# Second norm of an encoder layer: g applied to the gathered rows instead of before the split, half of the split on VectorE, the last residual ahead of it

## The reference

```
h = rmsnorm(x, norm_ffn_g)          # x * rsqrt(mean(x^2) + eps) * g
grp_logits = h @ w_grp + b_grp      # 4 groups, top 1
exp_logits = h @ w_exp + b_exp      # 8 experts in the group, top 2
y = sum over the chosen experts e of weight * ((silu(h @ w_gate[e]) * (h @ w_up[e])) @ w_down[e])
x = x + y;  out = rmsnorm(x, final_norm_g)
```

## Time and profile before

| | before |
|---|---|
| runs (us) | 861.05, 861.25, 862.1; median 861.25 |
| profiled execution, span from first to last instruction (us) | 857.0 |
| busy: TensorE, VectorE, ScalarE, GpSimd (us) | 763.1, 224.5, 163.3, 63.6 |
| mean granted TensorE clock (share of full) | 0.972 |
| moved by DMA | 238.90 MB |

### The profile page before, as it was taken

How to read it: one execution, slowest core, us unless ns; L and a number is a source line. 1 busy time by engine, 2 the same in 40 slices (tenths; PEclk the granted TensorE clock), 3 DMA queues, 4 the chain that set the end, 5 groups by cost and what they waited for, 6 DMA issues and landing times.

```text
span 857.0 us, 14144 instructions
## 1 busy us (share of the span) xinstructions
PE 763.1 (89%) x6112; PEld 378.4 (44%) x6112; DVE 224.5 (26%) x429; ACT 163.3 (19%) x315; POOL 63.6 (7%) x49
## 2 busy tenths in 40 slices
PE   6997999999999997799999999999999988988830
PEld 3443444464566555444444444444444334334310
DVE  3037544003355257411111111111111101111116
ACT  5244120014344254201010101010101000000004
POOL 0714000000000034100000000000000000000023
PEclk9999999999999998899999999999999999999975
DMA  9322020402450362499999999999999999999945
GB/s 330 77 98 98 1 99 1 148 1 81 177 216 2 117 275 99 169 395 417 420 420 416 420 419 418 420 418 418 419 417 420 419 417 421 418 418 420 416 169 227
DMA packets 54011, 238.90 MB, mean 279 GB/s; under 512 B 5856, under 2 KB 7264, under 8 KB 37600
## 3 DMA queue, kind: packets, MB, share of 16 engines
q1 hardware_dynamic: 47712, 225.93, 65.5%
q10 hardware_dynamic: 5120, 8.39, 2.6%
q0 software_dynamic: 1152, 4.19, 1.4%
HBM read 228.02 MB, written 10.49 MB: 278 GB/s over the span
## 4 chain that ended last, share of the span: by engine, by line
PE 58%; SPq 16%; DMA 14%; DVE 6%; ACT 3%; issue 2%; POOL 1%; POOLq 0%; ACTq 0%; DVEq 0%
PE bank L408 17%; SPq L321 13%; PE bank L700 13%; DMA arena<-in_w_up 9%; PE bank L719 7%; PE bank L690 6%; PE bank L569 4%; DMA arena<-in_w_down 3%; PE bank L620 3%; DVE arena L998 2%; SPq L332 2%; PE bank L603 2%; PE bank L511 1%; DMA arena<-rows_out,arena 1%; PE bank L587 1%
## 5 line engine op out<-in xcount | busy, mean ns | idle before, releaser
L700 PE MATMUL bank<-arena 128*64 128x512 f32 x1024 | 227.9, 594 | 14.0 <-DMA arena<-in_w_up 13.2
L408 PE MATMUL bank<-arena 128*128 128x512 f32 x384 | 171.0, 601 | 5.9 <-ACT arena L799 5.9
L700 PEld LDWEIGHTS bank<-arena 128*64 128x64 f32 x1024 | 73.5, 137 | 162.4 <-issue 137.7
L719 PE MATMUL bank<-arena 128*64 128x512 f32 x512 | 116.9, 598 | 15.7 <-ACT arena L952 15.1
L408 PEld LDWEIGHTS bank<-arena 128*128 128x128 f32 x384 | 72.2, 191 | 94.5 <-issue 90.5
L690 PEld LDWEIGHTS bank<-arena 128*128 128x128 bf16 x3072 | 92.3, 98 | 25.2 <-issue 25.2
L690 PE MATMUL bank<-arena 128*128 128x64 bf16 x3072 | 96.0, 194 | 0.0
L998 DVE TENSOR_TENSOR arena<-bank,arena 128x256 f32<-128x256 f32 (+1 forms) x80 | 30.3, 395 | 249.3 <-ACT arena L948 214.1
L719 PEld LDWEIGHTS bank<-arena 128*64 128x64 f32 x512 | 34.5, 136 | 77.6 <-issue 62.1
L948 ACT ACTIVATE arena<-bank 128x256 f32<-128x256 f32 x32 | 12.3, 384 | 284.8 <-PE bank L700 284.8
L1273 DVE COPY arena<-bank 128x512 f32<-128x512 f32 x32 | 22.1, 692 | 120.7 <-PE bank L719 120.7
(11 more groups left out here) (157 smaller groups left out, 506.0 us busy)
## 6 DMA issues: line engine op xcount, KB each, us to landing
arena<-in_w_gate SPq DMA_DIRECT2D x64, 1024.0 KB, 23.3
arena<-in_w_up SPq DMA_DIRECT2D x64, 1024.0 KB, 23.1
arena<-in_w_down SPq DMA_DIRECT2D x32, 2048.0 KB, 26.1
arena<-in_w_in SPq DMA_DIRECT2D x6, 2048.0 KB, 8.1
rows_out<-arena ACTq DMA_DIRECT2D x64, 128.0 KB, 6.1
arena<-in_x SPq DMA_DIRECT2D x4, 512.0 KB, 5.9
arena<-in_w_out SPq DMA_DIRECT2D x2, 1024.0 KB, 8.0
arena<-in_w_out SPq DMA_DIRECT2D x1, 2048.0 KB, 18.3
```

The costliest lines, as they stand in the source:

```text
L408: m = pe.matmul(pbank[n % UNIT_BANKS][:], lhs(k), rhs(k), start=(k == 0), stop=(k == KC - 1))
L700: mm = pe.matmul(pbank[s][64 * half:64 * half + 64, :].rearrange("p (g f) -> p g f", g=2), xT[:, k], wg_sb[s][:, :, k, half * 256:(half + ...
L719: mm = pe.matmul(pbank[5 + s][64 * half:64 * half + 64, :], hidT[:, kc % 2, kc // 2], wd_sb[s][:, kc, half * 512:(half + 1) * 512], start= ...
```

## The change

g is no longer multiplied into the rows before the split. The split works on x1 * rstd2 alone, and g, now laid out by chunk as gffn_pk (128 x 8, loaded in place of g2b), is multiplied in when the gathered rows leave PSUM (`rows_T_evict`; ScalarE does the same in the general path). hi is an Identity activation of x1 with scale rstd2; h2 as a tile is gone. The rest, x1 * rstd2 - hi, is made on VectorE by scalar_tensor_tensor, into rest2, which lies by chunk; mid and the last part read it in unit step. GpSimd keeps the last part alone. Tile 3 is split in two halves. On VectorE the order is new: rest(0), rest(1) between the first tiles' steps, route(0, 2) ahead of x1_T_evict(2), residual(3) and norm2(3) behind it, then rest(2). On TensorE router(1) stands ahead of out_proj(3, 0) and the numbers of keep_clock differ. The gather goes tile by tile, with one start flag for the bank. SP waits for the same number of parts as before.

```diff
-        h2 = [at(128 + 4 * i, D) for i in range(2)]
+        rest2 = [at(128 + 4 * i, KC, P) for i in range(2)]
...
-            sp.dma_start(g2b, g_ffn.broadcast_to((P, D))).then_inc(g2_in, 16)
+            sp.dma_start(gffn_pk, g_ffn.rearrange("l (p k) -> (l p) k", k=KC)).then_inc(g2_in, 16)
...
             router(0)
             x1_T(1)
             out_proj(2, 1)
+            router(1)
             out_proj(3, 0)
-            router(1)
             x1_T(2)
             out_proj(3, 1)
             router(2)
-            keep_clock(4)
             x1_T(3)
-            keep_clock(4)
+            keep_clock(3)
             router(3)
-            keep_clock(10)
+            keep_clock(12)
...
-                for k in range(KC):
-                    for t in range(TT):
+                for t in range(TT):
+                    for k in range(KC):
                         for i in range(3):
                             mm = pe.matmul(pbank[3][:, k * SLOTS:(k + 1) * SLOTS], h2_part[t][i][:, k], pick[s][:, t],
-                                           start=(t == 0 and i == 0), stop=(t == TT - 1 and i == 2))
+                                           start=(t == 0 and k == 0 and i == 0), stop=(t == TT - 1 and k == KC - 1 and i == 2))
...
-            def hi(t):
+            def hi(t, ks):
                 act.wait_ge(sumsq2_done, t + 1)
-                act.wait_ge(h2_done, t + 1)
-                nc.scalar.copy(h2_part[t][0], h2_by_chunk(t)).then_inc(hi_done, 1)
-
-            def mid(t):
-                act.wait_ge(rest_done, t + 1)
-                nc.scalar.copy(h2_part[t][1], h2_by_chunk(t)).then_inc(mid_done, 1)
-
-            for stage, t in ((square, 0), (square_root, 0), (square, 1), (x1_T_evict, 0), (hi, 0), (square_root, 1),
-                             (x1_T_evict, 1), (mid, 0), (hi, 1), (square, 2), (square_root, 2), (mid, 1), (x1_T_evict, 2),
-                             (hi, 2), (mid, 2), (square, 3), (x1_T_evict, 3), (square_root, 3), (hi, 3), (mid, 3)):
-                stage(t)
+                act.wait_ge(rstd2_done, t + 1)
+                nc.scalar.activation(h2_part[t][0][:, ks], x1_by_chunk(t)[:, ks], ACT.Identity,
+                                     scale=rstd2[:, t:t + 1]).then_inc(hi_done, 1)
+
+            def mid(t, ks, rests):
+                act.wait_ge(rest_done, rests)
+                nc.scalar.copy(h2_part[t][1][:, ks], rest2[t % 2][:, ks]).then_inc(mid_done, 1)
+
+            square(0)
+            square_root(0)
+            square(1)
+            x1_T_evict(0)
+            hi(0, all_k)
+            square_root(1)
+            x1_T_evict(1)
+            hi(1, all_k)
+            mid(0, all_k, 1)
+            mid(1, all_k, 2)
+            square(2)
+            square_root(2)
+            hi(2, all_k)
+            x1_T_evict(2)
+            square(3)
+            x1_T_evict(3)
+            square_root(3)
+            hi(3, halves[0])
+            mid(2, all_k, 3)
+            hi(3, halves[1])
+            mid(3, halves[0], 4)
+            mid(3, halves[1], 5)
...
-                dve.wait_ge(rstd2_done, t + 1)
-                if t >= 2:
-                    dve.wait_ge(parts_done, t - 1)
-                nc.vector.scalar_tensor_tensor(h2[t % 2], x1[:, t], rstd2[:, t:t + 1], g2b, ALU.mult, ALU.mult).then_inc(h2_done, 1)
...
+            def rest(t, ks, his):
+                dve.wait_ge(rstd2_done, t + 1)
+                dve.wait_ge(hi_done, his)
+                if t >= 2:
+                    dve.wait_ge(parts_done, t - 1)
+                nc.vector.scalar_tensor_tensor(rest2[t % 2][:, ks], x1_by_chunk(t)[:, ks], rstd2[:, t:t + 1],
+                                               h2_part[t][0][:, ks], ALU.mult, ALU.subtract).then_inc(rest_done, 1)
+
             residual(0)
             norm2(0)
             residual(1)
             x1_T_evict(0)
             norm2(1)
+            rest(0, all_k, 1)
             x1_T_evict(1)
+            rest(1, all_k, 2)
             residual(2)
             norm2(2)
+            route(0, 2)
             x1_T_evict(2)
-            route(0, 2)
             residual(3)
+            norm2(3)
+            rest(2, all_k, 3)
             x1_T_evict(3)
-            norm2(3)
+            rest(3, halves[0], 4)
+            rest(3, halves[1], 5)
             route(2, 4)
-            dve.wait_ge(mid_done, TT)
-            ks = slice(KC // 2, KC)
-            tt(h2_part[TT - 1][2][:, ks], h2_by_chunk(TT - 1)[:, ks], h2_part[TT - 1][1][:, ks],
-               ALU.subtract).then_inc(parts_done, 1)
...
-                nc.vector.tensor_copy(xT.rearrange("p k t -> p (k t)"), pbank[3][:]).then_inc(xt_evicted, 1)
+                tt(xT, pbank[3][:].rearrange("p (k t) -> p k t", k=KC), gffn_pk.unsqueeze(2).broadcast_to((P, KC, SLOTS)),
+                   ALU.mult).then_inc(xt_evicted, 1)
...
-            for t in range(TT):
-                pool.wait_ge(hi_done, t + 1)
-                nc.gpsimd.tensor_tensor(h2_by_chunk(t), h2_by_chunk(t), h2_part[t][0], ALU.subtract).then_inc(rest_done, 1)
+            for t in range(TT - 1):
                 pool.wait_ge(mid_done, t + 1)
-                ks = slice(0, KC if t < TT - 1 else KC // 2)
-                nc.gpsimd.tensor_tensor(h2_part[t][2][:, ks], h2_by_chunk(t)[:, ks], h2_part[t][1][:, ks],
-                                        ALU.subtract).then_inc(parts_done, 1)
+                nc.gpsimd.tensor_tensor(h2_part[t][2], rest2[t % 2], h2_part[t][1], ALU.subtract).then_inc(parts_done, 1)
+            for h in range(2):
+                pool.wait_ge(mid_done, TT + h)
+                nc.gpsimd.tensor_tensor(h2_part[TT - 1][2][:, halves[h]], rest2[(TT - 1) % 2][:, halves[h]],
+                                        h2_part[TT - 1][1][:, halves[h]], ALU.subtract).then_inc(parts_done, 1)
```

More of the change, by code:

```diff
@@ L138, in mixer_and_moe @@
         w_lr = at(206, KC, 2 * RANK)
-        g2b = at(199, D)
         gfb = at(128, D)
@@ L154, in mixer_and_moe @@
         b_r_sb = take(GROUPS + EXPERTS)
-        gffn = take(KC)
+        gffn, gffn_pk = take(KC), take(KC)
         ssq, root, rstd = take(TT), take(TT), take(TT)
@@ L242, in mixer_and_moe @@
         wo_done, x1_done, sumsq2_done, ms2_done = sem("wo_done"), sem("x1_done"), sem("sumsq2_done"), sem("ms2_done")
-        root2_done, rstd2_done, h2_done = sem("root2_done"), sem("rstd2_done"), sem("h2_done")
+        root2_done, rstd2_done = sem("root2_done"), sem("rstd2_done")
         xr_done, res_pool = sem("xr_done"), sem("res_pool")
@@ L276, in mixer_and_moe, with x1_by_chunk @@
         rows_out_d = rows_out.rearrange("(e t) (h d) -> e h t d", t=SLOTS, h=2)
-        def h2_by_chunk(t):
-            return h2[t % 2].rearrange("p (q k) -> p k q", k=KC)
+        def x1_by_chunk(t):
+            return x1[:, t].rearrange("p (q k) -> p k q", k=KC)
+        halves = [slice(0, KC // 2), slice(KC // 2, KC)]
+        all_k = slice(0, KC)
         block = ctx.enter_context(nc.Block())
@@ L973, in _ @@
                     act.wait_ge(a_T, c + 1)
-                    nc.scalar.copy(g_hT[c // 2][:, 4 * (c % 2):4 * (c % 2) + 4].rearrange("p a b -> p (a b)"),
-                                   pbank[0][:]).then_inc(a_copied, 1)
+                    for j in range(4):
+                        k = 4 * (c % 2) + j
+                        m = scaled_copy(g_hT[c // 2][:, k], pbank[0][:, j * P:(j + 1) * P], gffn_pk[:, k:k + 1])
+                    m.then_inc(a_copied, 1)
                 with act.Fori(0, EXPERTS) as e:
```

## The result

| | before | after |
|---|---|---|
| median (us) | 861.67 | **853.78** |
| runs of the comparison (us) | 861.05 to 863.12 | 852.0 to 854.14 |
| span of the profiled execution (us) | 857.0 | 852.1 |
| VectorE, GpSimd busy (us) | 224.5, 63.6 | 216.7, 55.0 |

The ratio is 0.9906, interval 0.9891 to 0.9921: faster by 0.9%, where 855.4 us against 861.25 was 0.7%. First the page of the kernel after: span, busy share of TensorE, and the head of the chain that ended last by line (L323 is the issue of w_gate and w_up, L321 in the earlier trace rows).

What follows compares the result with a forecast made beforehand. The start of the memory-bound expert weight stream was taken to set the end. 7.3 us won at residual(3) less 1.5 us given back on the tail is 5.8 us: 861.25 to 855.4 us, range 853.0 to 858.5 us.

Steps and rivals of the forecast that it cites:

- The bound: Expert weight stream: the end is its start plus a constant, so an earlier 359.06 us makes the end earlier by as much.
- The 4.25 us around the span: Outside the profiled span: median 861.25 us less span 857.0 us, taken as fixed.
- route(0, 2) free, and residual(3) earlier: Router stage, VectorE: route at 4.25 us with at most 0.1 lost; residual(3) 325.8 to 327.1 us, 7.3 us won.
- The order: Router stage: router(1) one out_proj, 3.4 us, earlier, so route(0, 2) follows at once; no separate gain was given.
- The tail: From last residual to both_b: 14.9 us instead of 13.4, so 1.5 us given back.
- The rule on turns between VectorE and GpSimd: VectorE instructions with two SBUF inputs and GpSimd ones reading SBUF exclude each other: gain 5.8 us, not 6.5.
- What cost nothing: Priced at 0: moved half subtract, load of g, eviction with g, gather tile by tile, clock keepers.
- The gather's order: Gather tile by tile, the same 96 matmuls: priced at 0, though no row showed this order.
- rival (d): Gather in every loop turn: new order costs TensorE time; at 2 us more each, 878 us; 5%.
- Rival (c): Routes held up as long as before, 9.4 us instead of 1.1, nothing left: 860 to 863 us; 5%.
- Rival (b): Routes catch more GpSimd subtracts, mid stays 2.07 us, or half clock lasts: stream 1.5 to 4 us later, 857 to 859.5; 15%.
- Rival (a): Stepped splits cost 1.28 us, 853.9 us, or clock stays at 2.4 GHz, gather ends 1.7 us earlier, 853.7 us; 15%.

Runs made afterwards that it cites:

- e5: Kernel after with 25 instead of 5 clock keepers between the rank matmuls and the first gather: median 856.74 us, ratio 0.9948.
- e1: Kernel before with the new order and keeper numbers alone; g, split and gather as before: median 863.89 us, ratio 1.0025.
- e2: Kernel after with the old order of router(1), route(0, 2) and x1_T_evict(2), and the old keeper numbers: median 855.14 us, ratio 0.9928.
- e10: Kernel after with GpSimd's last part of tile 2 computed twice in a row: median 856.74 us, ratio 0.9943.
- e3: Kernel after with the gather chunk by chunk, as in the kernel before: median 852.23 us, ratio 0.9906.
- e11: Kernel after with rest(2) ahead of norm2(3) on VectorE and, on ScalarE, mid(2) behind the second half of hi(3): median 853.99 us, ratio 0.9904.
- e4: Kernel after with VectorE's split reading x1 in unit step, which leaves mid and the last part without meaning: median 850.44 us, ratio 0.9883.
- e9: Kernel after with chunks as blocks of 128 consecutive features, so w_gate and w_up load in rows of 2 KB: median 877.03 us, ratio 1.0185.
- e6: Kernel after with 1 instead of 5 clock keepers behind the rank matmuls: median 853.03 us, ratio 0.9910.
- e7: Kernel after with 12 instead of 3 clock keepers ahead of router(3) and 24 instead of 12 behind it: median 853.45 us, ratio 0.9912.
- e8: Kernel after once more, unaltered: median 854.16 us, ratio 0.9917.

## Why the prediction was right, and where its sizes were off

**The bound: right.** The end is the start of the stream plus a constant. w_gate to end is 499.3 us after, 499.25 in e5 with w_gate 2.9 us later, 498.9 in e1 with w_gate at 69.56. The 4.25 us around the span were wrong: in after, time and span of the same execution are 854.14 and 852.1, so 2.0 us lie around it. By that the profiled execution of before would have taken about 859 us, less than any of those the median is from; the difference did not hang on it.

**route(0, 2) free, and residual(3) earlier: right, 0.4 us too small.** Forecast was an end of 327.1 us against a start of 292.26, 34.84; it was 34.40. I let two things end at 33.54 us from the start, the eviction of tile 2 and all of out_proj(3, 1). The eviction ended at 33.21, and the first of the two adds needs only out_proj(3, 0): it started at 33.13, before out_proj(3, 1) ended at 33.58. e2 shows that the bundle of the split frees route(0, 2). e10 shows, in the other route, that GpSimd's time alone, with no data in it, holds VectorE.

**The order: not worth what the text let it seem.** It was costed together with the split. Alone it costs 2.7 us (e1), with the split it brings 1.1 (e2).

**The tail: 0.6 us given back, not 1.5.** From the end of the last residual to both_b it took 14.01 us, against 14.9 forecast and 13.4 before. The terms that the rows size stand: split 2.05 to 2.09 us (taken 2.0), half 1.14 (1.09), hi 2.16 (2.1), mid 1.04 (1.06). Mis-sized was the turn of GpSimd's subtract within rest(3). Forecast: it waits for the first half, runs 2.34 us, and the second half ends 336.8 - 292.26 = 44.54 us from the start; measured 337.08 - 293.47 = 43.61. Of these 0.93 us, 0.36 are the first half's earlier end. Another 0.4 are the subtract's: it takes 2.14 us in unit step when alone (320.84 us), not L1405's 2.34, and it lost only 0.3 of the 0.5 us that it shares with the first half, since it stands from 333.75 us with 2.43 us in all. The last 0.2 are the second half's, which ended 0.90 us behind the subtract and not 1.1. And the CAST of route(2, 4) lost 0.81 - 0.17 = 0.64 us where I put 1.0. So at both_b it is these 0.93 us, of which 0.44 had been there since residual(3), and 0.4 us more in the route: 55.57 - 48.41 = 7.16 us gained instead of 5.8.

**The rule on turns between VectorE and GpSimd: the trace agrees.** The rows of before showed only VectorE held. After, it goes both ways: the subtract at 317.77 us took 3.11 us, beside rest(1), which ended at 318.94, and the next 2.14; the half at 336.15 us took 1.89, beside the second half of rest(3), and the next 1.15. Each lost 0.7 to 1.0 us to a neighbour that it lay beside for 0.9 to 1.2. That half of rest(3) took 2.19 instead of 1.14 us, beside the subtract. This is what the Trainium skill states (SBUF — State Buffer, "Who interferes with whom"): whichever of the two is first holds the other for a whole instruction. In the profile the held one is not shown as starting late, but as started and long. The five GpSimd subtracts took 10.7 us in all, where I had 9.4.

**From both_b to w_gate: 0.35 us less** than before (10.88 and 11.23); the forecast had nothing here. 0.13 of it lie in the ten keeper matmuls (2.35 and 2.48) and 0.18 in the gather (3.61 and 3.79), both partly at 1.2 GHz in both kernels. So this part is the clock of two executions and not the edit. With the full clock the stretch is 9.44 us.

**What cost nothing: right.** The eviction with g takes 692 ns, in the first gather and in the loop, and the plain copy of the gathered rows in before's loop, L1263, 692 too. The gather's order: nothing (e3). So rival (d) is out. Rival (c) is out by the free route(0, 2). Rival (b) did not come in after, and e10 and e11 show its mechanism: one more thing for GpSimd to do, or a route that starts 2.8 us earlier, and the adds lose 1.8 us. Of rival (a) neither condition held in after: the stepped split cost what was taken, and the clock was at 1.2 GHz behind the ranks. Both prices are about right. 1.38 us come back in unit step (e4), and the one layout tried that gives it costs the stream 24 us (e9). The gather runs at 2.4 GHz in e3, e5 and e6, which have the code of after up to the ranks, and behind e7's keepers; that is 1.45 us at w_gate, where I had priced 1.7, and its worth in the median is not shown. The wait for both_b that I took as some 4 us was 2.31.

## What to carry to other kernels

Look for small VectorE instructions that last 1 to 3 us. Here a GpSimd instruction held them each time, and what helped was less GpSimd work in that stretch; the new order alone made it worse (e1). Ahead of a stream that is bound by memory only its start counts, so measure each edit at the first load it lets go, from a mark that lies before all edits. Before a step in SBUF is made straight, see what the layout does to the length of the DMA's rows.

## What was not expected of the hardware

A held instruction shows as long, not as late, on GpSimd as on VectorE (2.14 and 3.11 us, 1.15 and 1.89 us). In route, CASTs of two columns (up to 2.53 us) and adds of 8 or 64 columns (2.96 and 2.51) are held for up to a whole subtract of 128 x 1024, while MAX8, FIND_INDEX8 and the scalar_tensor_tensor that reads PSUM keep their 0.24, 0.16 and 0.24 us in all fourteen profiles, in before also beside the subtract that stands from 323.07 to 325.74 us. A step of 32 bytes costs VectorE 2.05 against 1.28 us and ScalarE 2.16 against 1.15 for 128 x 1024. Rows of 2 KB instead of 8 stream at 396 against 419 GB/s. And the same code comes out in two ways. With the clock falling right behind a wait of 2.96 us (e3, e5, e6) it was back for the gather, 2.96 us in all three; with the clock falling later (after, e8) the gather took 3.6 and 3.5. The early fall alone does not secure it: e10 had it too, but after an idle of 2.46 us before the ranks its clock was down again and its gather took 3.17.
